# Half-angle root in the recurrence, head 0's scores behind the last query slab, first convolution tap on ScalarE: a two-layer hybrid block on one core

## What is computed

```
u = dwconv(r_u, conv_c, 4 taps) + conv_c_b                    # both sequences
r, i = sigmoid(u @ wa + ba), sigmoid(u @ wx + bx)             # 8 blocks, 2 directions
log_a = -8 * softplus(-lam) * r;  a = exp(log_a)
b = sqrt(-expm1(2 * log_a)) * (i * u);  h = linear_scan(a, b) # forward and backward
y_c = (gelu(r_g) * h) @ w_c_out
q, k = rotate(q, cos, sin), rotate(k, cos, sin)
y_b = softmax([q k_window, q k_ctx, sink]) @ v                # 8 heads, 2 kv heads, 2 blocks of 128
```

## Time and profile before

| | |
|---|---|
| median of 3 runs | 2160.63 us (2160.46 to 2161.41) |
| profiled execution, its own time | 2154.54 us |
| its span, first to last instruction | 2152.7 us |
| mean granted clock of TensorE | 0.993 |
| busy: PE, DVE, ACT, POOL | 96%, 52%, 42%, 38% |
| instructions | 30915 |

### The profile page before, as it was taken

How to read it: one execution, slowest core, us unless ns; L and a number is a source line. 1 busy time by engine, 2 the same in 40 slices (tenths; PEclk the granted TensorE clock), 3 DMA queues, 4 the chain that set the end, 5 groups by cost and what they waited for, 6 DMA issues and landing times.

```text
span 2152.7 us, 30915 instructions
## 1 busy us (share of the span) xinstructions
PE 2072.0 (96%) x11836; PEld 1720.3 (80%) x11836; DVE 1125.2 (52%) x2021; ACT 907.0 (42%) x1424; POOL 823.5 (38%) x348
## 2 busy tenths in 40 slices
PE   6999889999999999999999999999999999999997
PEld 4778677788877778776777778776889999899997
DVE  6894354577789532123111111489745886444555
ACT  4895333322222332233222212379755434544434
POOL 1003221344434334332333344400445887644443
PEclk9999999999999999999999999999999999999999
DMA  8212111222222222654534422421223555344443
GB/s 332 79 59 98 59 43 56 79 98 88 88 98 90 87 78 104 236 218 176 225 120 173 156 96 81 155 77 71 108 100 120 177 190 187 146 174 157 178 176 137
DMA packets 38699, 278.37 MB, mean 129 GB/s; under 512 B 4416, under 2 KB 4416, under 8 KB 5312
## 3 DMA queue, kind: packets, MB, share of 16 engines
q1 hardware_dynamic: 38592, 276.87, 35.1%
HBM read 275.80 MB, written 1.05 MB: 129 GB/s over the span
## 4 chain that ended last, share of the span: by engine, by line
PE 79%; DVE 9%; ACT 7%; issue 2%; DMA 2%; POOL 1%; SPq 0%; DVEq 0%; ACTq 0%; POOLq 0%
PE PS L441 76%; PE PS L524 2%; ACT WH L769 2%; DVE PS L1177 1%; ACT S L769 1%; DVE SM L1180 1%; ACT TMP L769 1%; ACT L769 1%; PE PS L681 1%; DVE WL L1174 1%; DVE ZL L1174 1%; ACT CD L769 1%; POOL WL L416 1%; DMA RAW<-in_stream 1%; DMA S<-in_modw 1%
## 5 line engine op out<-in xcount | busy, mean ns | idle before, releaser
L416 POOL TENSOR_TENSOR WL<-RAW,WH 128x1024 fp32r<-128x1024 f32 x344 | 823.3, 2413 | 1313.3 <-ACT WH L769 1313.3
L441 PE MATMUL PS<-HH,WH 128*128 128x512 f32 (+1 forms) x2272 | 807.7, 355 | 19.3 <-DVE HL L1177 7.3
L441 PE MATMUL PS<-HL,WH 128*128 128x512 f32 (+1 forms) x2272 | 780.2, 343 | 0.0
L441 PE MATMUL PS<-HH,WL 128*128 128x512 f32 (+1 forms) x2272 | 779.7, 343 | 0.0
L769 ACT ACTIVATE WH<-RAW 128x1024 fp32r<-128x1024 f32 x416 | 417.4, 1052 | 666.1 <-PE PS L441 626.4
L441 PEld LDWEIGHTS PS<-HH,WH 128*128 128x128 f32 x2272 | 430.2, 189 | 96.5 <-issue 30.0
L441 PEld LDWEIGHTS PS<-HL,WH 128*128 128x128 f32 x2272 | 430.5, 190 | 59.5 <-issue 7.9
L441 PEld LDWEIGHTS PS<-HH,WL 128*128 128x128 f32 x2272 | 429.7, 189 | 56.0
L441 PE MATMUL PS<-ZH,WH 128*128 128x512 f32 (+1 forms) x992 | 339.4, 342 | 10.7 <-DVE ZL L1174 7.1
L441 PE MATMUL PS<-ZL,WH 128*128 128x512 f32 (+1 forms) x992 | 336.1, 339 | 0.0
L441 PE MATMUL PS<-ZH,WL 128*128 128x512 f32 (+1 forms) x992 | 336.1, 339 | 0.0
(11 more groups left out here) (157 smaller groups left out, 1572.1 us busy)
## 6 DMA issues: line engine op xcount, KB each, us to landing
RAW<-in_stream SPq DMA_DIRECT2D x208, 1024.0 KB, 4.8
CD<-in_modw SPq DMA_DIRECT2D x42, 1024.0 KB, 7.4
CD<-in_lruw SPq DMA_DIRECT2D x2, 2048.0 KB, 9.3
X<-in_xT SPq DMA_DIRECT2D x2, 1024.0 KB, 6.3
S<-in_modw SPq DMA_DIRECT2D x2, 1024.0 KB, 10.9
G<-in_modw SPq DMA_DIRECT2D x2, 1024.0 KB, 20.8
RAW<-in_modw SPq DMA_DIRECT2D x1, 1024.0 KB, 15.8
TMP<-in_modw SPq DMA_DIRECT2D x1, 1024.0 KB, 17.8
```

Source lines behind the costliest of these rows:

```text
L416: nc.gpsimd.tensor_tensor(WL[:, a:b], RAW[:, a:b], WH[:, a:b].bitcast(F32), ALU.subtract)\
L441: return nc.tensor.matmul(out, lhs, rhs, start=start, stop=stop)
```

## The change

- **Half-angle root.** The root is written as sqrt(1 − a²) = (1 + a) · sqrt(tanh(−log_a / 2)). ACT takes the root of the tanh directly and no longer computes the second exponential (a², e0 and e1); DVE's `rests` becomes `sums`, which multiplies the driving term by 1 + a. The third column group of LC is dropped.
- **First tap.** Tap 0 of the 4-tap convolution with its bias moves from DVE to ACT (`Identity` with scale and bias), behind the copy of the slab out of PSUM.
- **Head 0.** `scores` of units 0 and 1 of head 0 stand behind the last q slab, ahead of the last two rotations; their maxima and probabilities move along, and the cast of the second d_in slab moves behind these probabilities. The rotations use banks 6 and 7 only. The scans of the recurrence's last block (n = 7) stand behind the first cosines, with their driving term in PSUM (`driven`).
- **Layer 0's heads 1 to 7.** No scores of the next head at step 14; the table is changed as shown.
- **Start.** Constants and parameters are loaded ahead of X, the first weight slab ahead of the modulation slabs, and ACT casts it ahead of the first root. DVE's loop over the heads of layer 1 is written out.

```
-ATTENTION = [[("t0", 6), ("t1", 9), ("o0", 9), ("t2", 13), ("o1", 13), ("n0", 14), ("o2", 16)],
+ATTENTION = [[("t0", 8), ("t1", 10), ("o0", 11), ("t2", 13), ("o1", 14), ("o2", 16)],
...
             sp.dma_start(CIN[:, :], cT).then_inc(in_loaded, 16)
+            sp.dma_start(CST[:, :], consts).then_inc(par_loaded, 16)
+            sp.dma_start(PRM[:, :], prm).then_inc(par_loaded, 16)
             for j in range(2):
...
-            sp.dma_start(CST[:, :], consts).then_inc(par_loaded, 16)
-            sp.dma_start(PRM[:, :], prm).then_inc(par_loaded, 16)
+            load(0, 0)
             for j, n in enumerate(MOD_ORDER):
                 sp.dma_start(MOD_HOMES[j], slab_of(modw, n)).then_inc(first_loaded[j // 2], 16)
-                if j == 1:
-                    load(0, 0)
...
-                        mm(bank(4 + 2 * s + t, NX), ROT, KR[t][:, 0:NX] if st_a is a["kv_a"] else QR[s][t], True, True).then_inc(st_p.sem, 1)
+                        mm(bank(6 + s, NX, t * NX), ROT, KR[t][:, 0:NX] if st_a is a["kv_a"] else QR[s][t], True, True).then_inc(st_p.sem, 1)
...
+                    if n == 3:
+                        for u in range(2):
+                            scores(0, u, 0, 0)
+                        pe.wait_ge(a["q_v"].sem, a["q_v"].at(0, "s1"))
                     rotate(a["q_a"], a["q_p"], n - 1, (n - 1) % 2)
...
+            act.wait_ge(par_loaded, 32)
+            decay(0)
...
             table(ACT.Sqrt)
+            high(0, 0)
             norm_root(0, "n1", 2)
...
+                    act.wait_ge(fa.sem, fa.at(n, "ru"))
+                    if n > 1:
+                        act.wait_ge(a["ci_p"].sem, n - 1)
+                        act.wait_ge(av.sem, av.at(n - 2, "iu1"))
+                    fn(seqs(tmp(s), 2), padded(n, 2, -(TAPS_C // 2)), ACT.Identity, scale=par(l, "conv_c", n),
+                       bias=par(l, "conv_c_b", n)).then_inc(fa.sem, 1)
...
-                        act.wait_ge(av.sem, av.at(n, f"w{d}"))
-                        fn(lru(n, 2 * d), lru(n, 2 * d), ACT.Sqrt).then_inc(a["ci_s"].sem, 1)
+                        act.wait_ge(aa.sem, aa.at(n, f"a{d}"))
+                        fn(lru(n, 2 * d), lru(n, 4 + d), ACT.Sqrt).then_inc(a["ci_s"].sem, 1)
...
-                    for d in range(2):
-                        act.wait_ge(aa.sem, aa.at(n, f"a{d}"))
-                        fn(lru(n, 2 * d), lru(n, 2 * d), ACT.Exp, scale=lc(1, n, d), bias=lc(1, n, d)).then_inc(aa.sem, 1)
...
+                    if n == 2:
+                        act.wait_ge(a["q_v"].sem, a["q_v"].at(0, "s0"))
+                        stage_q(0, 0)
+                        table(ACT.Exp)
...
+                for u in range(2):
+                    probs(0, u)
+                high(b + 2, 1)
...
+                def driven(n, d):
+                    return bank(4 + d) if n == KC - 1 else lru(n, 2 * d + 1)
...
-                        tt(lru(n, 2 * d + 1), lru(n, 2 * d + 1), lru(n, 2 * d), MUL).then_inc(ar.sem, 1)
+                        dve.wait_ge(av.sem, av.at(n, f"w{d}"))
+                        tt(driven(n, d), lru(n, 2 * d + 1), lru(n, 2 * d), MUL).then_inc(ar.sem, 1)
...
-                scans(KC - 1)
-                outputs(KC - 1)
-                for n in range(4):
...
+                for n in range(3):
+                    dve.wait_ge(tile_done[n % 2], 2 * (pair_base(l, "q") + n // 2) + 2)
+                    cosines(a["q_a"], a["q_v"], n, n % 2, lambda t: query(n, t))
                     if n == 0:
+                        scans(KC - 1)
+                        outputs(KC - 1)
                         z_out(KC - 1)
-                    turned(a["q_v"], a["q_p"], n, n % 2, lambda t: row(CD, 2 * n + t, NX))
+                    if n < 2:
+                        turned(a["q_v"], a["q_p"], n, n % 2, lambda t: query(n, t))
...
+                for u in range(2):
+                    maxima(0, u)
+                dve.wait_ge(tile_done[1], 2 * (pair_base(l, "q") + 1) + 2)
+                turned(a["q_v"], a["q_p"], 2, 0, lambda t: query(2, t))
+                cosines(a["q_a"], a["q_v"], 3, 1, lambda t: query(3, t))
+                turned(a["q_v"], a["q_p"], 3, 1, lambda t: query(3, t))
```

More of the change, by code:

```diff
@@ L716, in _ @@
                         done = steps
[L717 to L720, removed]
+                        if x and x[0] == "s":
+                            pe.wait_ge(a["q_v"].sem, a["q_v"].at(2, "s1"))
                             scores(n, 2, kv, s)
@@ L1014, in stage_q @@
                     fn(row(S, 2 + s, W), row(CD, n, W), ACT.Copy).then_inc(a["di_qs"].sem, 1)
-                def d_in(n, s, m, more=True):
[L1017 to L1029, removed]
+                for n in range(4):
+                    tiles(b + n // 2, n % 2)
+                    q_in(n, n % 2, b + n // 2)
+                    if n < 3:
+                        high(b + n // 2 + 1, n % 2)
+                    if n == 0:
+                        z_high(KC - 1)
+                    if n == 2:
+                        act.wait_ge(a["q_v"].sem, a["q_v"].at(0, "s0"))
+                        stage_q(0, 0)
+                        table(ACT.Exp)
@@ new lines, in probs @@
+                def probs(n, u):
+                    sm = 14 * u
+                    act.wait_ge(dv.sem, dv.at(n, f"n{u}"))
+                    if u < 2:
+                        fn(PR[u], bank(4 + u), ACT.Exp, scale=SCALE, bias=SM[:, sm + 4:sm + 5],
+                           accum_out=SM[:, sm + 6:sm + 7]).then_inc(da.sem, 1)
+                    else:
+                        for q in range(2):
+                            fn(PR[0][:, q * NC:(q + 1) * NC], bank(6, NC, q * NC), ACT.Exp, scale=SCALE,
+                               bias=SM[:, sm + 4 + q:sm + 5 + q], accum_out=SM[:, sm + 6 + q:sm + 7 + q]).then_inc(da.sem, 1)
+                    act.wait_ge(dv.sem, dv.at(n, f"f{u}"))
+                    q = 2 if u == 2 else 1
+                    fn(SM[:, sm + 8:sm + 8 + q], SM[:, sm + 8:sm + 8 + q], ACT.Exp).then_inc(da.sem, 1)
@@ L1284, in _ @@
                     inverse_root("n1", 2, tmp(1))
-                    for s in range(2):
-                        dve.wait_ge(x_loaded[s], 16)
                     nv, na, nh = a["n1_v"].sem, a["n1_a"].sem, a["n1_h"].sem
@@ L1526, in d_in_slab @@
-                    ahead = units == 3
+                    mx, mm_, nm, _, es, _, _ = scalars(u)
+                    dve.wait_ge(a["di_s"].sem, a["di_s"].at(n, f"s{u}"))
+                    if u < 2:
+                        far = bank(4 + u, P, (1 - u) * P)
+                        step(tt(far, far, TRI[u], ADD), f"k{u}")
+                        step(V.reduce_max(mx, bank(4 + u), AX.X), f"m{u}")
+                    else:
+                        step(V.reduce_max(mx, seqs(bank(6), 2), AX.X), "m2")
@@ L1527, in d_in_slab, with step @@
+                turned(a["q_v"], a["q_p"], 3, 1, lambda t: query(3, t))
+                def d_in_slab(n, s, m):
+                    def step(ins, name):
+                        ins.then_inc(dv.sem, 1)
+                        dve.wait_ge(dv.sem, dv.at(n, name))
                     for u in range(units):
-                        if u > 0 or not ahead or (isinstance(n, int) and n == 0):
-                            maxima(n, u, sink)
+                        if n > 0 or u == 2:
+                            maxima(n, u)
@@ L1540, in d_in_slab @@
                                 ts(h, h, SM[:, 14 * u + 12 + j:14 * u + 13 + j], None, MUL).then_inc(dv.sem, 1)
-                    if ahead and n + 1 < HEADS:
-                        maxima(n + 1, 0, par(l, "sink", n + 1))
                     dve.wait_ge(tile_done[s], 2 * m + 2)
@@ L1547, in _ @@
                 b = pair_base(l, "d_in")
-                if units == 3:
-                    for n in range(KC):
-                        d_in_slab(n, n % 2, n // 2 + b)
-                else:
-                    with dve.Fori(0, KC // 2) as i:
-                        for s in range(2):
-                            d_in_slab(2 * i + s, s, i + b)
+                for n in range(KC):
+                    d_in_slab(n, n % 2, n // 2 + b)
                 def conv_d(taps):
```

149 lines of the change are left out of this document (64 added, 85 removed).

## The result

The changed kernel takes 2123.14 us (median of 4 runs, 2121.03 to 2123.87) against 2160.61 us (4 runs, 2160.46 to 2161.41): a ratio of 0.9824, 95% interval 0.9807 to 0.9841, so 37.5 us less where 30.0 were forecast. The forecast of 2130.6 was 7.5 us too high: the result lies outside the forecast's own range (2126 to 2135), at the lower edge of the wide one (2123 to 2139).

What follows compares the result with a forecast made beforehand. PE was busy 96% of the span, so only its waits and low clock could be won. 12.9 + 3.1 + 5.0 + 9.6 + 1.1 − 1.7 = 30.0 us off the median 2160.63 gave 2130.6; own range 2126 to 2135, wide 2123 to 2139.

Steps and rivals of the forecast that it cites:

- Heads 1 to 7, the wait: Layer 0, transposes t0: PE's wait for q0 falls from 1.95 to 0.1 us, 7 x 1.85 = 12.9 us.
- and with it two half-clock stretches of this stage, 2 x 1.55: Layer 0, heads 1 to 7: two half-clock stretches go with the waits, 3.1 us gained.
- Prologue, 1.1: Start: ACT can start HH at 25.0 instead of 26.15; gain 1.1 us, between −2.5 and 1.5.
- It stood 6.1 us below the median …, and I take the difference from the median: Whole kernel: the 30.0 us gain is taken from the timed median 2160.63, not the profiled execution's 2154.54.
- Clock, −1.7: New waits of 2.5 and 2.5 to 3.5 us bring one more half-clock stretch, −1.7 us.
- Handover, layer 0: q stage to d_in: t0 at 236.9 instead of 241.9, gain 5.0 us despite a new 2.5 us wait.
- Layer 1: c_in and handover: t0 earlier by 9.1 to 11.4 us, 9.6 taken, c_in's 2.7 included.
- the held case at q0: Layer 1 handover: DVE doesn't slip in after POOL's first instruction, so t0 at 1565.1 instead of 1562.8.
- (a): Rival, both handovers: DVE slips between POOL's instructions, late casts cost nothing; about 37 us, 2124; chance 0.14.
- (b): Rival, heads 1 to 7: DVE's chain is later, about 1 us of wait stays; 2139; chance 0.15.
- (c): Rival, layer 0 heads: DVE work on PSUM is held too, waits of 4.7 us; about 2176; chance 0.03.
- (d): Rival, heads: casts and POOL shift along, wait stays 1.95, only handovers gain; about 15 us, 2146; chance 0.07.

Runs made afterwards that it cites:

- second pair: one more profiled execution each of the kernel before and the changed kernel, no edit; stage gains sum to 37.1 us; timed medians 2160.75 and 2122.53 us.
- the kernel before again: kernel before, unedited, timed and profiled again: 2160.75 us (12 runs); that profiled execution 2161.05 us.
- the recurrence's part: kernel before with only the half-angle root and the first tap on ACT, without `driven` or the new cosine order: 2153.28 us, ratio 0.9968.
- the start's part: kernel before with only constants first, weight slab ahead of modulation slabs, ACT's decay and first cast ahead of modulation rows: 2154.95 us, ratio 0.9979.
- step 5: changed kernel with t0 of layer 0 after step 5 instead of 8: 2143.53 us (6 runs).
- first pair: the profiled executions of the result, kernel before (2154.54 us) and changed kernel (2122.59 us); stage gains sum to 31.9 us.
- the heads' part alone: kernel before with only the new table and no scores issued a head ahead: 2139.65 us, ratio 0.9907.
- Step 7: changed kernel with t0 of layer 0 after step 7 instead of 8: 2130.92 us (4 runs).
- the scans in SBUF: changed kernel with the last block's driven input left in SBUF instead of PSUM: 2126.37 us (4 runs).

## Why the prediction was off, point by point

The step that failed is the way from the profile to the median: stretches and start were priced as one quick execution showed them, and the difference to the median was taken as the same for both kernels. The mechanisms of the waits were right. The second pair stands 7.1 us above the forecast: 3.1 in heads 1 to 7, 2.8 at the start, 2.7 behind the handovers (the clock term's place), less 1.5 in the other rows.

- *Heads 1 to 7, the wait.* Right: 1.95 to nothing, q0 bound to POOL's end, a margin of 0.05 us where I had 0.1. The period fell by 2.05 us, not 1.85: 14.4 us, not 12.9.
- *"and with it two half-clock stretches of this stage, 2 x 1.55"*. This is the first term that failed. Two of seven is one draw (the prediction says two of eight at 1.95, but the eighth wait, head 0's, is 0.77); four further executions of programs with such waits had 3, 3, 1 and 2 stretches there (the kernel before again, the recurrence's part, the start's part, step 5). The mean is close to two, so the term was not far off for an average execution; in the second pair it was 3 x 1.55. With the longer period that makes 19.1 us against 16.0.
- *Prologue, 1.1*. The second. It was right for the first pair (0.7). In the execution that I read no stretch stood near 30 us, behind the modulation slabs; of the five profiled executions with the old start three have it in the record and a fourth, the heads' part alone, runs at half speed there without one in the record. It is 1.5 of the 3.9 in the second pair. Another 1.6 are the kernel after's own: its first matmul stands at 17.72 us in the first profile and at 16.36 in the second. The smaller wait (1.94 beside 2.56) is no difference in loading: both end at the same time (23.45 and 23.36), but PE, at half speed, ended the matmuls ahead of it at 21.51 and not at 20.80. The part alone is worth 4.8 timed, 1.7 of it shown at the start.
- *"It stood 6.1 us below the median …, and I take the difference from the median"*. This is the step behind both. It assumes that what sets the profiled execution apart from the median is the same in both kernels. It is not: of the 6.5 us between the two profiled executions of before, 3.6 lie at places that the change edits (1.5 at the start, −1.0, 1.6 and 1.5 from the handover of layer 0 to that of layer 1), as stretches at waits that it takes away, and had to be counted as gain. Another 3.1 lie in the part whose code is the same in both kernels and are plain spread. With the second execution's 19.1 and 3.9 in place of 16.0 and 1.1 the sum is 35.9.
- *Clock, −1.7*. The first profile after shows no stretch at head 0 of either layer, the second shows one in layer 1. Its timeline there, and the window around it with a granted clock of 0.94:

```profile
1539.93 1.04 PE L670 MATMUL PS<-CST,TMP 128*128 128x128 f32 x4 [3.05 <-DVE TMP L1191]
...
1530.00:1560.00 30.00, 26.95 (x184) 24.14 (x184) 17.88 (x53) 14.34 (x31) 14.12 (x6) 0.94 0.30 106
```

Step 7, step 5 and the scans in SBUF have one at that wait as well, so four of five executions pay the term, and its mechanism was right. What it cost stands in the row of layer 1, not behind it: the −1.4 and 1.0 of the last row lie in the part whose length varies by 4 us with the same code.

- *Handover, layer 0.* Right: 4.5 to 5.5 for 5.0, with a new wait of 1.80 (I had 2.5) from the held 128x2 instruction.
- *Layer 1.* Right: 2.2 for 2.7 in c_in, 6.6 to 6.8 for 6.9 at the handover, and the held case at q0 (3.10, I had up to 3.5), 2.1 of it POOL's.
- *Rivals.* (a) names a time of 2124 that came out, but not for its reason: neither handover slips between POOL's two instructions, and the late casts cost 3.8 us. (b) did not happen: heads 1 to 7 have no wait at t0. (c) did not happen: reductions from PSUM pass. (d) did not happen.

What stays open: why a given wait of 2 us is followed by a stretch in one execution and not in another, why the kernel after reached its first matmul 1.4 us earlier the second time, and the few microseconds by which the part behind the attention of layer 1 varies.

## What to carry to other kernels

Before subtracting a modelled gain from a median, compare the profiled execution with the spread of the timed ones: if it is a quick one, ask which waits in it got away without a half-clock stretch, and price each wait that the change removes with the stretches that usually follow, here 1.95 us of wait plus 0.2 to 0.7 us (one to three stretches of 1.55 us over seven heads). The record alone doesn't always show a stretch at the very start; compare there how long equal matmuls take. An engine that holds another can be cured from either side: moving the consumer by two steps or the cast by half a slab gave the same 20 us. When work is moved into a gap, list what the moved instruction sets off on the third engine; one late cast cost 3.8 us of a 41 us gain.

## What the runs showed of the hardware that I had not expected

- The clock's cost of a wait is a matter of size and of chance: no stretch after 0.62 us (seven waits), two of seven after 2.00, one to three of seven after 1.95, in otherwise equal code. A stretch costs about 1.55 us here.
- The granted clock of a profile can read 1.00 over the first microseconds of PE's work while equal matmuls take twice their later time (sixteen in 1.93 us at 25.15, thirty-two in 1.93 at 32.14).
- Behind layer 1's attention the spacing of 128x256 matmuls differs between two executions of one program: 1,206 of them took 144.9 us in the first profile of before and 146.4 us in the second, at the full granted clock and with no wait over 0.2 us in either. It is spread over all of them, not in single gaps.
